# Four small constants allocated in front of the split weights of a stack of transformer layers

## The reference, cut to what matters

```
h = h + mixer(rmsnorm(h))                        # w_in 1024 x 2048 or 3784, w_out 1024 x 1024
h = h + memory_cross_attn(rmsnorm(h), mem_n)     # wq, wkv, wo
h = h + peer_ffn(rmsnorm(h))                     # u[eid], v[eid] of 16384 x 1024 each, 2 layers
h = h + ffn(rmsnorm(h))                          # gate and up 1024 x 2816 each, down 2816 x 1024, 2 layers
```

## Time and profile before

| | us |
|---|---|
| median of three timed runs | 2838.16 |
| lowest, highest | 2835.47, 2839.52 |
| span of the profiled execution (no other time of it is shown) | 2841.9 |

### The profile page before, as it was taken

The page is one execution under the profiler, slowest core; times in us unless marked ns, Lnnn a source line. Parts: engine busy times, 40 slices in busy tenths (PEclk is TensorE's granted clock), DMA queues, the critical chain, the costliest instruction groups (busy, mean ns, idle before and its releaser), DMA issues.

```text
span 2841.9 us, 57248 instructions
## 1 busy us (share of the span) xinstructions
PE 2768.2 (97%) x19552; PEld 2600.4 (92%) x19552; DVE 2048.3 (72%) x4430; ACT 1454.4 (51%) x2378; POOL 179.7 (6%) x141
## 2 busy tenths in 40 slices
PE   7999999999999999989999999999999999999998
PEld 7999899999988888979999999988888889999998
DVE  8657987886567677876698888566677876666665
ACT  5455445444455555555544444455555565446444
POOL 0004000000000000000275000000000000000000
PEclk9999999999999999999999999999999999999999
DMA  5445565455766665424456554676666525553454
GB/s 191 177 152 180 202 221 203 170 180 191 239 247 242 241 242 187 148 82 156 151 179 217 184 181 168 211 251 242 244 241 240 190 90 178 188 217 125 173 190 178
DMA packets 140452, 546.19 MB, mean 192 GB/s; under 512 B 15785, under 2 KB 81593, under 8 KB 83617
## 3 DMA queue, kind: packets, MB, share of 16 engines
q1 hardware_dynamic: 63216, 455.38, 44.4%
q10 hardware_dynamic: 73728, 67.14, 7.6%
q0 software_dynamic: 3376, 21.88, 2.0%
HBM read 505.53 MB, written 40.91 MB: 192 GB/s over the span
## 4 chain that ended last, share of the span: by engine, by line
PE 80%; DVE 12%; DMA 3%; ACT 2%; issue 2%; POOL 2%; SPq 0%; DVEq 0%; ACTq 0%
PE bank L796 24%; PE bank L797 23%; PE bank L798 23%; PE bank L1016 4%; DVE wL L551 3%; DMA ring<-in_w_stream 2%; POOL wL L551 2%; PE bank L917 1%; PE bank L937 1%; ACT wH L540 1%; PE bank L928 1%; DVE pr_m L1973 0%; DVE pr_eq L1969 0%; DVE pr_eq L1971 0%; PE bank L893 0%
## 5 line engine op out<-in xcount | busy, mean ns | idle before, releaser
L551 DVE TENSOR_TENSOR wL<-ring,wH 128x1024 fp32r<-128x1024 f32 x809 | 988.3, 1224 | 632.9 <-ACT wH L540 623.0
L540 ACT ACTIVATE wH<-ring 128x1024 fp32r<-128x1024 f32 x864 | 907.4, 1055 | 407.4 <-DMA ring<-in_w_stream 230.2
L796 PE MATMUL bank<-hnH,wH 128*128 128x256 f32 x3528 | 1020.0, 289 | 21.4 <-DVE wL L551 14.6
L797 PE MATMUL bank<-hnL,wH 128*128 128x256 f32 x3528 | 1002.4, 284 | 0.0
L798 PE MATMUL bank<-hnH,wL 128*128 128x256 f32 x3528 | 1002.3, 284 | 0.0
L796 PEld LDWEIGHTS bank<-hnH,wH 128*128 128x128 f32 x3528 | 680.8, 193 | 30.4 <-issue 15.1
L797 PEld LDWEIGHTS bank<-hnL,wH 128*128 128x128 f32 x3528 | 681.2, 193 | 0.5 <-issue 0.2
L798 PEld LDWEIGHTS bank<-hnH,wL 128*128 128x128 f32 x3528 | 680.4, 193 | 0.0
L796 PE MATMUL bank<-wH,wgtH 128*128 128x512 f32 x1024 | 398.5, 389 | 0.0
L797 PE MATMUL bank<-wL,wgtH 128*128 128x512 f32 x1024 | 398.4, 389 | 0.0
L798 PE MATMUL bank<-wH,wgtL 128*128 128x512 f32 x1024 | 398.3, 389 | 0.0
(11 more groups left out here) (411 smaller groups left out, 3530.6 us busy)
## 6 DMA issues: line engine op xcount, KB each, us to landing
ring<-in_w_stream SPq DMA_DIRECT2D x432, 1024.0 KB, 4.9
act_parked<-act_out ACTq DMA_DIRECT2D x256, 128.0 KB, 2.6
act_in<-act_parked ACTq DMA_DIRECT2D x256, 128.0 KB, 2.8
sw_bias<-in_c_swa POOLq DMA_DIRECT2D x1, 4096.0 KB, 15.5
relb_rows<-rel_table POOLq DMA_DIRECT2D x1, 2048.0 KB, 9.7
h_parked<-h POOLq DMA_DIRECT2D x2, 1024.0 KB, 5.9
h_back<-h_parked POOLq DMA_DIRECT2D x2, 1024.0 KB, 6.2
od_relb<-relb_rows POOLq DMA_DIRECT2D x2, 1024.0 KB, 7.6
```

Of the source, the lines that this page charges most:

```text
L540: eng.activation(wH[:, b % NBUF, :], raw(b), ACT.Copy).then_inc(w_high, 1)
L551: eng.tensor_tensor(wL[:, b % NBUF, :], raw(b), wH[:, b % NBUF, :].bitcast(F32), ALU.subtract).then_inc(w_low, 1)
L796: pe.matmul(dst, lh, rh, start=start, stop=False, skip_group_check=True)
L797: pe.matmul(dst, lh, rl, start=False, stop=False, skip_group_check=True)
```

## The change

The allocations of `vec`, `lbv`, `snk` and `rb` are moved from behind `act_out` to in front of `wH`. Nothing else is edited; the same tensors have the same sizes, and every instruction has the same operands at new addresses.

```diff
         hnH, hnL = sb("hnH", [P, DC, T], F32R), sb("hnL", [P, DC, T], F32R)
         ring = sb("ring", [P, SLOTS, 2 * BLK])
+        vec, lbv, snk, rb = sb("vec", [P, NVEC]), sb("lbv", [P, 24]), sb("snk", [P, 16]), sb("rb", [32, 8])
         wH, wL = sb("wH", [P, NBUF, BLK], F32R), sb("wL", [P, NBUF, BLK], F32R)
         act_out = sb("act_out", [P, 2, T])
         root_sb, mem_root = act_out[:, 0, :], act_out[:, 1, :]
-        vec = sb("vec", [P, NVEC])
         con = sb("con", [P, NCST])
         iww = sb("iww", [P, DC, 8])
-        snk = sb("snk", [P, 16])
-        rb = sb("rb", [32, 8])
         slotT = sb("slotT", [P, 3, T])
         small = sb("small", [P, 96])
         eps = small[:, 80:81]
-        lbv = sb("lbv", [P, 24])
```

## The result

The changed kernel is slower: 2850.6 us, median of 5 runs (2847.3 to 2854.1), against 2838.2 us for the kernel before in the same runs (2835.5 to 2841.5). The ratio is 1.0036, with its 95% interval from 1.002 to 1.0052. The forecast was 2797, with a range up to 2839. The profiled span went from 2841.9 to 2851.9 us.

A forecast was written before the change was run, and what follows sets the result against it. TensorE's matmul pace in the three split-operand products was taken as the bound; 39.5 + 9.1 − 0.2 = 48.4 us, times 0.85, gives 41 us off the 2841.9 us profile, 2797 us on the median; range 2780 to 2839.

The forecast's parts named there:

- Step (a): 256-column products with weights wH or wL, rows formerly at distance 0: pace 120.0 to 116.7 ns, 39.5 us saved.
- the row of ycat: Profile row of ycat's products, already at distance 288 from the weights: 116.7 ns per matmul, taken as (a)'s new pace.
- rival "no change": Paces come from absolute place or surroundings, not distance; hn keeps 120.0 ns, 2829 to 2842 us, say 2837; chance 0.12.
- Step (b): 512-column products with wH and wL as moving rows, distance becoming +224: 2.8 ns less each, 9.1 us saved.
- The bound of ±13 ns: Limits for (b): the 13.1 ns over the columns could all go (−43 us) or double (+43 us).
- the nearest rows: Basis of (b)'s choice: two other distances at 256 columns, 3.3 and 2.2 ns below distance 0; middle 2.8 ns.
- rival of the 512-column stage: 512-column products slow as wH and wL move: 43 us added if overhead doubles, 2848 us; chance 0.09.
- two signs named for a wrong forecast: The forecast is wrong if hn's pace stays, or if the 512-column pace rises above 236 ns.
- Step (c): att_OT, od_h and od_y, 1152 matmuls going from distance 64 to 352: −1.3 to +2.5 us, taken as 0.
- Step (d): Copies into wH and subtractions into wL: at most 24 ns more each, covered by other work; 21 us without cover.
- Step (e): Share of the saving reaching the end: 0.85 of 48.4 us, so 41 us; waits for wL grow a few us from 24.4.

The follow-up runs named there:

- the kernel of distances: Matmuls alone, not the computation: moving tiles 32 bytes apart against two weight tiles; 113.3 to 120.0 ns at 256 columns, 226.8 to 234.3 at 512.
- the kernel in which only the weights' products moved: Against the kernel before, the four constants stand in front of hnH, so hn and w move together; 2859.4 us, ratio 1.0067.
- the kernel with rows at 192: The kernel before with snk in front of wH and the shared area behind wL, so hn stands at 192 from the weights; 2824.1 us, ratio 0.9943.

## Why the prediction was wrong

**Step (a)** held. The distance changes the pace, and the change put hn at one where 256 columns take 116.9 ns, as the row of ycat had said (116.7). It brought 35 us at the pace, forecast 39.5; the missing part is a pace of 117.8 in parts of the feed-forward stage, and the matmuls next to a wait, which are counted in the rest. The rival "no change" falls. That the two reads of TensorE don't concern each other, which the page "SBUF — State Buffer" of the Trainium skill states in "Who interferes with whom", the kernel of distances speaks against: nothing else is at work there, and with the distance the pace goes from 113.3 to 120.0 ns. The 109 ns worked out from "TensorE: Matmul & The Clock Gate", "Back-to-back issue gap", was reached by no steady stretch of such products. The section gives that sum for an isolated matmul; for a stream of weight loads and matmuls it gives about 131 ns at 512 columns, and no run here shows that either: the least is 226.7 ns.

**Step (b)** failed, and in sign. It said that 512-column products gain 2.8 ns at +224, by the middle of two rows with 256 columns; they lose 6.6, 226.7 to 233.3 ns. Instead of −9.1 us it was +22 us with hn's own 512-column products. The two widths have different curves: at 512 columns all seven distances other than 0 cost 2.1 to 7.5 ns, at 256 columns none costs anything to speak of. The bound of ±13 ns held this value; the choice within it, "the nearest rows", did not. The rival of the 512-column stage named the right mechanism and mis-sized it at 13.1 ns, with a turning point at 10: by its working 6.6 ns would still have left a gain. So neither of the two signs named for a wrong forecast came: hn's pace changed, and 233.3 ns is below 236.

**Step (c)** went to its upper bound: att_OT, od_h and od_y run at 120.0 ns, +2.5 us.

**Step (d)** held: the mean subtraction takes 1224 ns in both kernels and the copy 1055; the kernel in which only the weights' products moved, with wL at its new place, has 25.8 us of waits for wL against 24.4.

**Step (e)** is the other failure. It took 0.85 of the saving to reach the end, as if each saved nanosecond on the chain counted and the rest were lost in proportion. With the measured paces this gives 0.85 × −11 = −9 us; the span grew by 10. The waits for wL were to grow by a few us and grew by 15.3. What was left out is that copies and subtractions run at their own pace and TensorE, coming earlier, finds the block not ready. In the gate and up products of the feed-forward, one step is two blocks. VectorE's subtractions for a step follow each other every 5.56 us in both kernels (starts at 2465.28 and 2470.84 us before, 2464.94 and 2470.50 after), while TensorE's 48 matmuls took 48 × 120.0 = 5.76 us before and 48 × 117.8 = 5.65 us after. The room that lets the splits catch up sank from 0.20 to 0.09 us per step, and so by half; that this room decides about the wait is my reading, and no run changes it alone. I read the cover of the splits from busy shares (140 of 200 us), and in the one-hot stage, where no wait came; the waits came at the starts of stages and in the feed-forward, where the chain from ScalarE to VectorE is long and not dense. By stretches the waits for wL grew from 8.9 to 13.0 us in the first 110 us, from 6.0 to 8.9 up to 480, from 5.0 to 5.4 between 1000 and 1900, from 4.0 to 6.5 between 1900 and 2440, and from 0.5 to 5.8 in the feed-forward stages behind; from 480 to 1000 us there are none in either kernel. That waits grow because of the pace is shown by three comparisons in the table: a faster hn brings them on in three layouts, the new place of wL without a faster hn does not, and lighter subtractions take most of them away. How they grow with the saving is not settled.

The sum, as it should have read: −35 (a) + 22 (b) + 2.5 (c) − 0.5 (one-hot and others) + 21 (waits) = +10 us.

## What to carry to other kernels

Where a steady product runs some nanoseconds above what its columns take, try the distance between its moving and its weight tile, modulo 256 bytes, and measure each width by itself, in the kernel too, since one distance can have several paces; the best distance of one is not that of another, and a tile that is moving in one stage and weights in the other has two to serve. Before a gain in pace is counted, ask how much room the producers have at each stage's start, from the intervals at which they deliver and not from their busy share: here 17 us of waiting came back for 28 saved. Then the producers are the next thing to make lighter; with half the subtraction gone, 40 of 49 us reached the end of the profiled span, against 21 of 45 with all of it.

## What the runs showed of the hardware

- The pace of products in float32r, with a load of 128 columns of weights for each, depends on the distance of the two operands modulo 256 bytes: 113.3 to 120.0 ns at 256 columns, 226.7 to 234.3 ns at 512 (the kernel of distances).
- At one distance there can be two steady paces, 113.3 and 117.8 ns at 192 and at 320, and which it is goes with the number of products before the run; in the kernel with rows at 192 it changes from one block to the next. At 288 three were seen: 116.7, 117.8 and, for ff_a in one stage, 120.0 ns.
- A pause of 2.4 us was followed by 3.4 us at 1.2 GHz and cost 1.5 us beyond itself.
- The same kernel loses more or less to half the clock from run to run: the mean granted clock of the kernel before lay between 0.988 and 0.994, its time between 2849.0 and 2835.1 us. A difference of 13 us of half clock between two single profiles (20.4 and 7.2 us) can't be put down to their layouts.
